# Modulation rows of a two-network kernel: w_mod slabs multiplied on GpSimd ahead of time and kept in a 16-row table

## The chip, the cores and the metric

One NeuronCore of a Trainium2 chip runs the whole program. The metric is the device time of one execution in microseconds (us). The kernel works in fp32; many matmuls take their operands as fp32r, split into a high and a low part.

## What is computed

The reference chains two blocks over x of 256 tokens by 1024. The first block (hgrn/forgetting attention, differential attention, two mixtures of 32 experts) is not touched. The second block has two layers (MLA and GQA attention, then Hyena), each steered by modulation rows, which are what the change is about:

```python
silu_c = jax.nn.silu(c)                                # c: 1024 numbers
for i in range(2):
    m_l = silu_c @ w_mod[i] + b_mod[i]                 # w_mod[i]: 1024 x 6144
    sh1, sc1, g1, sh2, sc2, g2 = split(m_l, 6)         # six rows of 1024
    hl = rmsnorm(x, norm1_g[i]) * (1 + sc1) + sh1
    ol = mixer(hl)                                     # attention (0), Hyena (1)
    x = x + g1 * ol
    x = x + g2 * mlp(rmsnorm(x, norm2_g[i]) * (1 + sc2) + sh2)
x = rmsnorm(x, final_g)
```

w_mod is 24 slabs of 1024 x 512 (2 MB each, 50 MB in all) that serve one matrix-vector product each. In layer 0 the context tokens get a shift and scale of their own too.

## The kernel before

Weights pass through a ring of six SBUF slots (`RING`), a slab of 128 x 4096 fp32 each: `view_k` shows it as 8 tiles of 128 x 512, tile k holding rows 128k to 128k+127 of the weight. SyncE (SP) loads slabs in a written-out order (lines 680 to 786). Slab n goes to slot n mod 6 and its load waits until the last PE unit that reads slab n - 6 has filled its bank (`plan.last_reader`). A unit is one filling of one of the eight PSUM banks; `make_plan` (line 181) hands out banks in turn, and PE waits before each filling (`claim`) until the bank's last filling is drained.

The names: mod0.pre1 are four slabs (shift and scale of layer 0's first norm), mod0.gate1 two (g1), mod0.pre2 four (shift and scale of the second norm), mod0.gate2 two (g2); mod1 likewise. A slab is worked in one of two ways. `c_product` (line 956) lets PE multiply the 8 tiles by a widened c. The other way is `multiply_c` (line 2050) and `sum_up` (line 961): DVE multiplies tile 0 by a column of silu(c) and adds the seven others, multiplied, one after the other (8 instructions of 128 x 512, each waiting for the last) into a buffer `partial`; then one PE matmul with a matrix of ones sums over the 128 partitions and puts the row into all of them:

```python
tell(mm(banks[u.bank][:, :], ones, partial[name][i], start=True, stop=True), u)
```

`add_bias` (line 2035) adds that to the bias row in shift, scale or gate, which GpSimd's queue has loaded before. mod0.pre1 has to serve two different c and is worked both ways. Of mod1.pre1 the first two slabs go by `c_product`, the other two by DVE.

Where this stands in the order: after the attention, DVE's program (from `turn("turn.a_out", xT3)` on) multiplies gate1's two slabs and pre2's first two, adds the gate's bias, multiplies pre2's last two, and goes into `modulated_after` (line 2001): multiply each 128 x 512 result of the projection by gate, add to h, add both biases, then the norm of two tiles. PE meanwhile projects a_out[0], sums gate1, projects a_out[1], sums pre2 (lines 1365 to 1371). Layer 1 does the same round hyena_out. gate2's two slabs are multiplied by DVE inside the MLP, a slab in two halves. mod1.pre1 comes after layer 0's MLP.

The attention stages that the change reaches: PE projects mla_cq, mla_ckv, gqa_q and gqa_kv, waits for DVE's `lora_ready` (lines 1308 and 2555), transposes, projects mla_q and mla_kv, waits for `mla_qk` (lines 1331 and 2593), and goes through 16 steps of MLA and 16 of GQA (`attend`, line 928; `full_attend`, line 2158). Each step has logits, turned probabilities and an output. In Hyena, PE makes filters, six hyena_in projections with transposes, and twice a DFT, a product on DVE and an inverse DFT.

GpSimd issues small loads (bias rows, gains, tables, lines 796 to 860) and computes nothing.

## Time and profile before

| | us |
|---|---|
| median of 3 runs (2672.91 to 2678.48) | 2678.41 |
| the profiled execution, its own time | 2672.54 |
| its span, first to last instruction | 2670.5 |
| PE, DVE, ACT busy in it | 2363.5, 1976.6, 1341.9 |
| mean granted TensorE clock | 0.933 |

Times below are us from the span's start in that execution. A row of the timeline has its start, its duration, the engine, the line of the kernel, the operation, what it writes and reads, and the count of instructions merged in it; in brackets is how long the engine had stood idle before it and what released it. PE is TensorE's matmuls, SPq the queue of SyncE. A fp32 matmul leaves two records.

### The profile page before, as it was taken

The page shows a single profiled execution, that of the slowest core. Times are in us where ns is not written, and L with a number is a line of the kernel's source. Part 1 is how long each engine was busy: PE and PEld are TensorE (multiplying, and loading weights), DVE is VectorE, ACT ScalarE, POOL GpSimd, SP SyncE. Part 2 cuts the span into 40 slices and gives each one's busy share as a digit, 9 for nine tenths or more (in the row PEclk, how much of TensorE's full clock was granted, in tenths as well). Part 3 has the DMA queues.
Part 4 walks back from the last instruction along what each step waited for, and adds up shares of the span by engine and source line. Part 5 has one row for each costly group of instructions (what it writes and reads, how often), then busy time and mean ns, then how long its engine had stood idle before and what let it go on. Part 6 is the DMA issues. An engine that isn't in the chain of part 4 may idle for free.

```text
span 2670.5 us, 29901 instructions
## 1 busy us (share of the span) xinstructions
PE 2363.5 (89%) x10986; PEld 1734.1 (65%) x10986; DVE 1976.6 (74%) x2443; ACT 1341.9 (50%) x1477; POOL 23.9 (1%) x45
## 2 busy tenths in 40 slices
PE   7996999999988869999999987897999568876998
PEld 6556777777764537777777754563887226733887
DVE  3747999999984649999999983458775644369775
ACT  3235888888861427888888831351432011101432
POOL 0000000000000000000000000000000000000000
PEclk9997999999999978999999997899899678988999
DMA  8314998888883217988888882306465501307370
GB/s 321 126 63 163 380 368 360 360 361 361 361 343 104 95 63 279 365 361 360 361 360 361 361 290 93 131 1 227 167 254 196 190 32 63 126 8 262 133 275 16
DMA packets 116505, 607.80 MB, mean 228 GB/s; under 512 B 5300, under 2 KB 8428, under 8 KB 91644
## 3 DMA queue, kind: packets, MB, share of 16 engines
q1 hardware_dynamic: 111536, 588.83, 56.8%
q0 software_dynamic: 4880, 17.76, 1.9%
q8 instruction: 60, 0.98, 0.2%
q14 instruction: 29, 0.24, 0.0%
HBM read 605.51 MB, written 1.05 MB: 227 GB/s over the span
## 4 chain that ended last, share of the span: by engine, by line
PE 54%; DVE 22%; issue 13%; ACT 9%; DVEq 1%; DMA 0%; POOL 0%; SPq 0%; ACTq 0%
PE bank L900 10%; DVE slab_parts L2393 6%; ACT high L1695 5%; PE bank L912 4%; PE bank L1174 4%; PE bank L1126 3%; PE bank L1153 3%; PE bank L999 3%; PE bank L1115 3%; PE bank L1387 2%; PE bank L1389 2%; PE bank L1388 2%; PE bank L1400 2%; PE bank L1402 2%; PE bank L1401 2%
## 5 line engine op out<-in xcount | busy, mean ns | idle before, releaser
L2393 DVE TENSOR_TENSOR slab_parts<-ring,high 128x2048 fp32r<-128x2048 f32 x384 | 862.3, 2288 | 41.8 <-ACT high L1695 37.9
L1695 ACT ACTIVATE high<-ring 128x2048 fp32r<-128x2048 f32 x384 | 727.6, 1914 | 44.6 <-PE bank L1126 35.7
L1126 PE MATMUL bank<-high,xT_parts 128*128 128x512 f32 x1024 | 294.3, 409 | 17.9 <-DVE slab_parts L2393 14.1
L1126 PE MATMUL bank<-slab_parts,xT_parts 128*128 128x512 f32 x1024 | 279.0, 394 | 0.0
L1538 ACT ACTIVATE arena<-bank 128x512 f32<-128x512 f32 (+4 forms) x162 | 89.4, 586 | 357.7 <-PE bank L900 98.8
L900 PE MATMUL bank<-ring,xT 128*128 128x512 f32 (+3 forms) x576 | 237.7, 574 | 11.1 <-DVE xT L2025 7.1
L1126 PEld LDWEIGHTS bank<-high,xT_parts 128*128 128x128 f32 x1024 | 184.7, 190 | 78.7 <-DVE slab_parts L2393 38.5
L1126 PEld LDWEIGHTS bank<-slab_parts,xT_parts 128*128 128x128 f32 x1024 | 193.5, 189 | 45.5
L1701 ACT ACTIVATE arena<-bank 64x512 f32<-64x512 f32 (+2 forms) x352 | 184.7, 534 | 62.8 <-PE bank L1153 52.1
L900 PEld LDWEIGHTS bank<-ring,xT 128*128 128x128 f32 x576 | 111.0, 194 | 134.5 <-issue 122.9
L1558 ACT ACTIVATE high<-ring 128x2048 fp32r<-128x2048 f32 x64 | 121.8, 1912 | 87.7 <-PE bank L1402 82.2
L2612 DVE TENSOR_TENSOR slab_parts<-ring,high 128x2048 fp32r<-128x2048 f32 x64 | 146.1, 2291 | 20.7 <-ACT high L1558 20.3
L1153 PE MATMUL bank<-high,hidden_parts 128*128 128x512 f32 x512 | 151.3, 417 | 7.0 <-DVE hidden_parts L2415 4.7
L1387 PE MATMUL bank<-xT_parts,high 128*128 128x256 f32 x512 | 148.1, 289 | 10.2 <-DVE slab_parts L2612 10.2
L1389 PE MATMUL bank<-xT_parts,slab_parts 128*128 128x256 f32 x512 | 145.7, 285 | 0.0
L1388 PE MATMUL bank<-xT_low,high 128*128 128x256 f32 x512 | 145.5, 284 | 0.0
L1153 PE MATMUL bank<-slab_parts,hidden_parts 128*128 128x512 f32 x512 | 141.5, 398 | 0.0
L1143 PEld LDWEIGHTS bank<-arena 128*128 128x128 f32 x1024 | 121.8, 192 | 5.9 <-ACT arena L1701 3.1
L1143 PE MATMUL bank<-arena 128*128 128x64 f32 x1024 | 123.0, 273 | 2.3 <-ACT arena L1701 2.3
L1701 ACT ACTIVATE xT_parts<-bank 128x512 fp32r<-128x512 f32 x128 | 76.3, 598 | 85.3 <-PE bank L1115 83.8
L1174 PE MATMUL bank<-arena 128*128 128x512 f32 x256 | 115.2, 592 | 2.7 <-DVE arena L2423 2.7
L885 PE MATMUL bank<-resident,arena 128*128 128x128 f32 x208 | 43.3, 384 | 83.6 <-DVE arena L1970 39.2
(361 smaller groups left out, 3679.1 us busy)
## 6 DMA issues: line engine op xcount, KB each, us to landing
ring<-in_moe_w_gate SPq DMA_DIRECT2D x64, 2048.0 KB, 8.5
ring<-in_moe_w_up SPq DMA_DIRECT2D x64, 2048.0 KB, 9.2
ring<-in_moe_w_down SPq DMA_DIRECT2D x64, 2048.0 KB, 8.8
ring<-in_mlp_w SPq DMA_DIRECT2D x32, 2048.0 KB, 13.4
ring<-in_w_mod SPq DMA_DIRECT2D x24, 2048.0 KB, 8.0
ring<-in_even_w_in SPq DMA_DIRECT2D x7, 2048.0 KB, 21.5
ring<-in_odd_w_in SPq DMA_DIRECT2D x6, 2048.0 KB, 10.1
ring<-in_h_w_in SPq DMA_DIRECT2D x6, 2048.0 KB, 7.9
```

The source lines that it names most:

```text
L900: last = mm(banks[u.bank][:, 0:n], lhs(k, tile), w[:, k, c0:c0 + n], start=(k == 0), stop=(k == k_tiles - 1))
L1126: last = mm(dst[:, :], seated2[:, 4 * half + k, e], part_[:, k, :], start=(half == a == k == 0), stop=(half == a == 1 and k == 3))
L1143: last = mm(dst[:, (4 * w + f) * SEATS:(4 * w + f + 1) * SEATS], raw[:, w, f * P:(f + 1) * P], fold, start=True, stop=True)
L1153: last = mm(dst[:, :], hidden2[:, f], part_[:, f, :], start=(a == f == 0), stop=(a == 1 and f == 3))
L1174: ins = mm(banks[bank][:, :], weightedT[:, (j // 2) * P:(j // 2 + 1) * P], pair_y[:, (j % 2) * 512:(j % 2 + 1) * 512], start=first, stop=last)
L1387: mm(dst, w_high[:, k, fs], xT_high[:, k, :], start=(k == 0), stop=False)
L1388: mm(dst, w_high[:, k, fs], xT_low[:, k, :], start=False, stop=False)
L1389: last = mm(dst, w_low[:, k, fs], xT_high[:, k, :], start=False, stop=(k == KD - 1))
L1695: act_fn(hi, weight_half(layer, name, half), ACT.Copy).then_inc(sem(f"high{layer}"), 1)
L1701: act_fn(dst, src(banks[u.bank]), func).then_inc(done or moe_drained[layer][u.bank], 1)
L2393: v.tensor_tensor(low, w, hi.bitcast(F32), ALU.subtract).then_inc(sem(f"low{layer}"), 1)
L2612: v.tensor_tensor(w_low, loaded, w_high.bitcast(F32), ALU.subtract).then_inc(sem("mlp_low"), 1)
```

## The change

Of the 24 slabs the four of mod0.pre1 stay as they are. The other twenty are split in two groups, mods_a (12) and mods_h (8), and are loaded and multiplied long before their rows are used. GpSimd multiplies a slab in the ring, in place: 8 multiplications of 128 x 512 by a column of silu(c), then sums of the first half and the second half of the tiles (4, 2 and 1 tiles wide), every instruction waiting for the one before. DVE does this for mod0.gate1's two slabs by the old chain, its result now in the slab's tile 0. PE then takes two slabs together (`collect`): a matmul with a 16-column one-hot matrix puts each slab's sum into its own row of a 16 x 512 PSUM tile, and DVE adds that tile to the table `mod_rows` (`keep`). Where the row is used, `spread` copies table row n to all partitions with one matmul.

The six collects of mods_a stand: before the wait for lora_ready, before the wait for mla_qk, after MLA steps 7 and 14, after GQA step 9, and before the transposes ahead of layer 0's MLP. The four of mods_h: before hyena_in, after its round 4, and after each DFT. The slabs' slots are freed by their collects, and the load order and GpSimd's program change with it. In `modulated_after` the biases and the scale now come ahead of the projection's results. mod1.pre1's c_products and the widening of c before them are gone.

```diff
+MODS = {"mods_a": tuple((name, i) for name, n in (("mod0.gate1", 2), ("mod0.pre2", 4), ("mod0.gate2", 2), ("mod1.pre1", 4))
+                        for i in range(n)),
+        "mods_h": tuple((name, i) for name, n in (("mod1.gate1", 2), ("mod1.pre2", 4), ("mod1.gate2", 2))
+                        for i in range(n))}
+ON_VECTOR = (("mod0.gate1", 0), ("mod0.gate1", 1))
+HYENA_SLABS = ("hyena_in", "hyena_in", "mod1.gate1", "mod1.gate1", "mod1.pre2", "hyena_in", "hyena_in", "hyena_in",
+               "hyena_in", "mod1.pre2", "mod1.pre2", "mod1.pre2", "mod1.gate2", "mod1.gate2")
+SUMS_AT = {("mla", 7): 2, ("mla", 14): 3, ("gqa", 9): 4}
...
         @block.sync
...
-            for name in ("gqa_q", "gqa_kv", "mla_q", "mla_kv", "mod0.gate1",
-                         "a_out", "mod0.pre2"):
+            for name in ("gqa_q", "gqa_kv", "mla_q", "mla_kv", "mod0.gate1", "mod0.pre2", "mod0.gate2", "mod1.pre1",
+                         "a_out"):
                 stream(name)
...
         @block.gpsimd
...
+                    for k in range(KD):
+                        link(nc.gpsimd.tensor_scalar(w[:, k], w[:, k], silu_c[:, k:k + 1], None, ALU.mult))
+                    for n in (4, 2, 1):
+                        link(nc.gpsimd.tensor_tensor(w[:, 0:n], w[:, 0:n], w[:, n:2 * n], ALU.add))
...
             load("rope2d_loaded", rope2d, A["rope2d"])
+            pool.wait_ge(sem("c_silu"), 1)
+            multiply_c("mods_a")
             pool.wait_ge(sem("gqa_o"), 16)
             load("bias0_gate1", gate, A["b_mod"][0, 2 * D:3 * D].partition_broadcast(P))
...
             gain_row(8)
+            multiply_c("mods_h")
             gain_row(9)
...
         @block.tensor
...
+            def collect(group, g):
+
+                u = U[group][g]
+                claim(u)
+                for a in range(2):
+                    n = 2 * g + a
+                    name, i = MODS[group][n]
+                    if (name, i) in ON_VECTOR:
+                        pe.wait_ge(sem(name + ".partial"), i + 1)
+                    else:
+                        pe.wait_ge(sem("mod_step"), POOL_STEPS * (ON_POOL.index((name, i)) + 1))
+                    last = mm(banks[u.bank][0:16, :], hot[:, 15 - n:31 - n], view_k(slab_ap(K[name][i]), KD, 512)[:, 0],
+                              start=(a == 0), stop=(a == 1))
+                tell(last, u)
+
+            def spread(u, name, i):
+
+                n = MODS[MOD_GROUP[name]].index((name, i))
+                drained(pe, U[MOD_GROUP[name]][4 if name in ("mod0.gate1", "mod0.pre2") else -1])
+                claim(u)
+                tell(mm(banks[u.bank][:, :], ident[0:16, n:n + 1].to_broadcast([16, P]), mod_rows, start=True, stop=True), u)
...
+            pe.wait_ge(sem("hot_ready"), 1)
+            collect("mods_a", 0)
             pe.wait_ge(sem("lora_ready"), 1)
...
+            collect("mods_a", 1)
             pe.wait_ge(sem("mla_qk"), 1)
...
                 if i == 0:
                     for k in range(2):
-                        sum_up(U["mod0.gate1"][k], "mod0.gate1", k)
-            for k in range(4):
-                sum_up(U["mod0.pre2"][k], "mod0.pre2", k)
+                        spread(U["mod0.gate1"][k], "mod0.gate1", k)
+                    for k in range(4):
+                        spread(U["mod0.pre2"][k], "mod0.pre2", k)
...
-            pe.wait_ge(sem("c_wide_ready"), 2)
-            for i in range(2):
-                c_product(U["mod1.pre1"][i], K["mod1.pre1"][i], 0)
-            for i in range(2, 4):
-                sum_up(U["mod1.pre1"][i], "mod1.pre1", i - 2)
+            for i in range(4):
+                spread(U["mod1.pre1"][i], "mod1.pre1", i)
...
         @block.vector
...
             def modulated_after(name, gate, bias):
 
                 g = gain_row()
+                add_bias(bias, [shift, scale], bias.replace("mod", "bias").replace(".", "_"), 2)
+                link(v.scalar_tensor_tensor(scale, scale, 1.0, g, ALU.add, ALU.mult))
...
+            def keep(group, g):
+
+                u = U[group][g]
+                full(dve, u)
+                if g == 0:
+                    drain(v.tensor_copy(mod_rows, banks[u.bank][0:16, :]), u)
+                else:
+                    drain(v.tensor_tensor(mod_rows, mod_rows, banks[u.bank][0:16, :], ALU.add), u)
...
             tell(v.tensor_copy(stat[:, 165:166], z_ckv[:, 0:1]), "lora_ready")
+            for i in range(2):
+                multiply_c("mod0.gate1", i)
+            keep("mods_a", 0)
             dma_done(dve, "rope2d_loaded")
...
             turn("turn.a_out", xT3)
-            for i in range(2):
-                multiply_c("mod0.gate1", i, i)
-            for i in range(2):
-                multiply_c("mod0.pre2", i, i)
             add_bias("mod0.gate1", [gate], "bias0_gate1", 1)
-            for i in range(2, 4):
-                multiply_c("mod0.pre2", i, i)
             modulated_after("a_out", gate, "mod0.pre2")
```

## Rows read from the trace of the kernel before

**Rows 1.** The page, busy time, share of the span and instructions of each engine

```profile
PE 2363.5 (89%) x10986; PEld 1734.1 (65%) x10986; DVE 1976.6 (74%) x2443; ACT 1341.9 (50%) x1477; POOL 23.9 (1%) x45
```

**Rows 2.** Timeline of DVE, layer 0's output projection

```profile
1818.81 0.49 DVE L2058 TENSOR_SCALAR rows<-ring,small 128x512 f32<-128x512 f32 x1
...
1824.84 0.49 DVE L2058 TENSOR_SCALAR rows<-ring,small 128x512 f32<-128x512 f32 x1
...
1842.94 1.41 DVE L2043 TENSOR_TENSOR arena<-arena,bank 128x512 f32<-128x512 f32 x2
...
1857.90 0.69 DVE L2010 TENSOR_TENSOR arena<-bank,arena 128x512 f32<-128x512 f32 x1
...
1862.40 2.86 DVE L2043 TENSOR_TENSOR arena<-arena,bank 128x512 f32<-128x512 f32 x4
1865.29 1.22 DVE L2015 SCALAR_TENSOR_TENSOR arena<-arena,gain 128x1024 f32<-128x1024 f32 x1
...
1869.33 0.16 DVE L1962 RECIPROCAL stat<-stat 128x1 f32<-128x1 f32 x1
...
1872.10 0.15 DVE L1980 COPY stat<-gain 128x1 f32<-128x1 f32 x1
```

**Rows 3.** Timeline of PE, the same stretch

```profile
1819.40 13.97 PE L900 MATMUL bank<-ring,xT 128*128 128x512 f32 x32 [0.99 <-ACT xT L1538]
1833.21 1.88 PE L965 MATMUL bank<-rows,resident 128*128 128x512 f32 x4
...
1857.29 3.75 PE L965 MATMUL bank<-arena,resident 128*128 128x512 f32 x4 [6.75 <-DVE arena L2010]
```

**Rows 4.** Waits in layer 0's MLP, 1876 to 2066: us, times, longest

```profile
PE bank L1387 <- DVE slab_parts L2612: 5.1, 1, 5.1
```

**Rows 5.** Timeline of PE, MLA steps 7 and 8 (outputs)

```profile
1749.38 1.00 PE L952 MATMUL bank<-arena 128*128 128x64 f32 x8
...
1751.58 1.00 PE L952 MATMUL bank<-arena 128*128 128x64 f32 x8
```

**Rows 6.** Groups of DVE instructions, 2100 to 2230: count, busy us, mean ns

```profile
L2700 DVE RECIPROCAL rows<-rows 128x1024 f32<-128x1024 f32 x2 | 13.1, 6552 | 10.8 <-ACT rows L1869 10.8
...
L2696 DVE TENSOR_TENSOR arena<-arena 128x2048 f32<-128x2048 f32 x4 | 9.2, 2293 | 12.4 <-PE bank L1442 12.3
```

**Rows 7.** Line 2060, multiply_c: ns min/median/max, first and last start

```profile
L2060 DVE SCALAR_TENSOR_TENSOR arena<-ring,small,arena x84: 750/752/753, 1575.8 to 2449.8; 128x512 f32<-128x512 f32 x84
```

**Rows 8.** Timeline of PE, the transposes after lora_ready

```profile
1699.45 1.54 PE L1313 MATMUL bank<-resident,arena 128*128 128x128 f32 x6 [9.00 <-DVE stat L2555]
```

**Rows 9.** Stretches, PE's sums of rows 3 after their wait

```profile
core 0: us, PE busy (x) PEld busy (x) DVE busy (x) ACT busy (x) POOL busy (x), PEclk, DMA share, GB/s
...
1857.30:1861.00 3.70, 3.70 (x4) 1.08 (x4) 3.53 (x7) 0.01 (x1) 0.00 (x0) 0.50 1.03 408
```

**Rows 10.** Timeline of SyncE's queue, slab loads

```profile
1713.69 121.80 SPq L689 DMA_DIRECT2D ring<-in_w_mod  x4
```

**Rows 11.** The page, DMA issues: count, size, median us to landing

```profile
ring<-in_w_mod SPq DMA_DIRECT2D x24, 2048.0 KB, 8.0
```

**Rows 12.** Timeline of DVE, mod1.pre1

```profile
2069.80 0.14 DVE L2656 COPY stat<-stat 128x1 f32<-128x1 f32 x1
...
2090.32 1.22 DVE L2668 SCALAR_TENSOR_TENSOR arena<-arena,gain 128x1024 f32<-128x1024 f32 x1
```

**Rows 13.** DMA issues, 2070 to 2072

```profile
arena<-in_b_mod POOLq DMA_DIRECT2D x2, 512.0 KB, 5.1
```

**Rows 14.** Timeline of PE, hyena_in and the first inverse DFT

```profile
2230.86 27.79 PE L912 MATMUL bank<-xT,ring 128*128 128x256 f32 x128
...
2351.11 3.78 PE L1487 MATMUL bank<-arena 128*128 128x512 f32 x4 [7.26 <-DVE xT L2746]
```

**Rows 15.** Groups of instructions, DVE, 2325 to 2412

```profile
L2743 DVE TENSOR_TENSOR arena<-rows 128x512 f32<-128x512 f32 x8 | 5.5, 692 | 0.3
```

More of the change, by code:

```diff
@@ L169, in mlp @@
             if j in GATE_SUMS:
-                self.sum_up(gate, GATE_SUMS.index(j), (0,))
+                self.take(gate, 1, (0,))
             if j < MLP_STEPS:
@@ L228, in make_plan @@
     p.stream("mla_kv", 1, 8)
+    for name, _ in MODS["mods_a"]:
+        p.vector_slabs(name, 1)
+    p.take("mods_a")
     p.take("mla_qT", 4)
@@ L239, in make_plan @@
         if i == 0:
-            for k in range(2):
-                p.sum_up("mod0.gate1", k)
-    p.vector_slabs("mod0.pre2", 4)
-    for k in range(4):
-        p.sum_up("mod0.pre2", k)
+            p.take("mod0.gate1", 2)
+            p.take("mod0.pre2", 4)
+    p.take("mods_a")
     p.take("turn.n2_0", 4)
     p.mlp("mlp0", "mod0.gate2")
-    p.stream("mod1.pre1", 2, 1)
-    p.vector_slabs("mod1.pre1", 2)
-    for k in range(2, 4):
-        p.sum_up("mod1.pre1", k)
+    p.take("mod1.pre1", 4)
     p.take("turn.n1_1", 4)
+    p.slab("filter_w4", None)
+    for name in HYENA_SLABS:
+        p.slab(name, None)
     p.take("filter_mlp", 3)
@@ L271, in make_plan @@
         if i == 0:
-            for k in range(2):
-                p.sum_up("mod1.gate1", k)
-    p.vector_slabs("mod1.pre2", 4)
-    for k in range(4):
-        p.sum_up("mod1.pre2", k)
+            p.take("mod1.gate1", 2)
+            p.take("mod1.pre2", 4)
     p.take("turn.n2_1", 4)
     p.mlp("mlp1", "mod1.gate2")
+    p.read_by_sums()
     return p
@@ L602, in build @@
         gate = at(14336, 1024)
-        two, four = [rows[:, 512 * i:512 * (i + 1)] for i in range(2)], [at(16384 + 512 * i, 512) for i in range(4)]
-        partial = {"mod0.pre1": four, "mod0.gate1": two, "mod0.pre2": four, "mod0.gate2": two, "mod1.pre1": four,
-                   "mod1.gate1": two, "mod1.pre2": four, "mod1.gate2": two}
+        four = [at(16384 + 512 * i, 512) for i in range(4)]
+        partial = {"mod0.pre1": four}
+        mod_rows = routers[0:16, 0:512]
+        hot = w_fox_f[:, 0:31]
         silu_c = small[:, 464:472]
```

107 lines of the change are left out of this document (61 added, 46 removed).

## Prediction

> **What bounds the kernel now.** I read the page first: TensorE (PE) is busy for 89% of the span and VectorE (DVE) for 74%, GpSimd (POOL) for 1% [rows 1]. An average says little here, so I then read the timelines of the stages that the change touches. In layer 0's output projection DVE starts the first w_mod slab at 1818.81 and the second at 1824.84: 6.03 us a slab, six slabs, 36.2 us, and the normalised tiles are ready at 1872.10 [rows 2]. PE projects a_out within the same time, then stands 6.75 us for DVE [rows 3]. So DVE sets the end there, and layer 1 repeats the pattern. In the two MLPs it is otherwise: PE waits once, 5.1 us at the start, and never again in 190 us [rows 4], so the two slabs that DVE multiplies inside each MLP cost nothing now and their removal gives nothing. In the attention steps PE has no gap: step after step begins 2.20 us apart [rows 5]. Whatever is put on PE there costs its full time.
>
> **Step 1, price of a slab on GpSimd.** Eight multiplications of 128x512 and sums of 128x2048, 128x1024 and 128x512, each waiting for the one before. The trace has no such work on POOL. Lower bound: DVE's price for the shapes, 8 x 0.49 + 2.29 + 1.22 + 0.69 = 8.1 us, 8.6 with gaps of 0.04. Upper bound: every element at the dearest DVE rate, the reciprocal's 6552 ns for 1024, or 6.4 ns; 7680 elements make 49 us [rows 2, 6]. The true value I expect near the lower end, since these are ordinary additions: I take 0.75 us, DVE's row for 512 elements of two operands [rows 7], for each multiplication, and twice DVE's time for each sum, 6.0 + 8.4 = 14.4, rounded to T = 14.
>
> The Trainium skill's page "GPSIMD Engine Reference" (section 3.1, Elementwise) gives 4497 ns for GpSimd's 128x2048 sum and 769 ns for a 512-element loop; by it a slab would be about 14.2 us, an estimate, and no run here shows it.
>
> **Step 2, the two DVE slabs before the attention.** DVE now tells lora_ready and PE, after 9.00 us of waiting, transposes at 1699.45 [rows 8]. The changed PE first needs table sum 0, whose two slabs DVE multiplies after lora_ready: 12.1 us. The two one-hot matmuls are like two ones-matmuls, 1.88 us for four records at full clock (2.4 GHz) and 3.75 us at granted clock 0.50 (the 1.2 GHz level), after a 6.75 us wait [rows 3, 9]. Behind a 21 us wait they should be slow: 3.75. Together +15.9. The DVE work up to mla_qk follows the same delay (its 0.7 us copy of the sum into the table included), and table sum 1 ends as that is ready. So the attention begins 16 us late.
>
> **Step 3, table sums inside the attention, and the wait for GpSimd.** The third and fourth pre2 slabs go into slots freed by mla_q and mla_kv. The first is issued at 1713.69 now [rows 10], after the change at 1729.6, and lands 8.0 us later [rows 11], 1737.6. GpSimd had been idle, so from there it works slab after slab: slab k is done at 1737.6 + kT. Table sum 2 (after MLA step 7, 1750.4 + 16 = 1766.4) needs two: 1765.6, just in time; it ends at 1768.3. Table sum 3 (after step 14) is reached seven steps on, 1768.3 + 15.4 = 1783.7, and needs four: 1793.6. PE waits 10 us; the sum ends at 1795.5. From the end of step 14 now (1765.8) to the start of the a_out projection at 1819.40 are 53.6 us [rows 3, 5]; with 1.9 for table sum 4 (slab 6 is done at 1821.6, PE comes at 1827) the projection starts at 1851.0: **+31.6**. In general this is 4T - 24.4, but not under 21.6 (T up to 11.5). GpSimd's queue also carries the loads of gate, shift and scale, now behind slab 8: 1849.6, landed by 1857, before they are needed at 1867. A return to full clock after the 10 us wait: +2.
>
> **Step 4, layer 0's output projection.** The chain of six slabs goes. PE: a_out's first half 14.0, six spreads at 0.86 = 5.2. Its second half would follow, but it reuses banks that DVE drains only after the gate and both modulation adds (1.4 + 2.9) and scale's 1.22: it starts about 22 us after the first instead of 15.5, and takes 13.9. Then two adds (1.4), two tiles of normalising at 2.78 [rows 2]: 1819.4 + 21.9 + 13.9 + 1.6 + 5.6 = 1862.4 against 1872.10, **-9.7**. Table sum 5 stands in PE's wait before the transposes: 0, and 1.9 if that wait were gone.
>
> **Step 5, mod1.pre1.** Now DVE has the MLP's result at 2069.80, and reaches the scale at 2090.32 [rows 12], after widening c, two slabs and the c_products. After: the same 2069.80, then the bias loads, which GpSimd issues at that point and which land 5.1 us after the issue [rows 13]; with two issues of about 1 us behind one another I take 2076.5. Four adds (2.9): scale at 2079.4. **-10.9**.
>
> **Step 6, layer 1.** Table sums 0 and 1 of mods_h stand in a gapless run of PE (27.8 us and more): +3.8. Sums 2 and 3 stand before the inverse DFTs, where PE waits 7.26 us for DVE [rows 14]: 0, given GpSimd is done, for which it has about 35 us for the first two slabs, from the landing of their loads on, and 74 for four; cover gone, 1.9 each. DVE's four table adds fall in its waits but the last: 0.2. The output projection as in step 4: **-9.7**. Loads: the slabs come in an order that leaves each hyena_in slab at least 15 us ahead of its use: 0; if one came late, its 8 us landing would show.
>
> **Step 7, both engines at the SBUF.** No row has GpSimd and DVE computing together. Lower bound 0: DVE's steps beside DMA traffic into the ring hold 750 to 753 ns [rows 7]. Upper bound: every two-input DVE instruction beside GpSimd doubles, some 20 us before the attention (1691 to 1711) and in the Hyena stage 11 us (products of two SBUF tiles as in line 2743, four groups of eight, half of them beside GpSimd) and 6 us of the convolution: 37 [rows 15]. I take 7, near the undisturbed rows.
>
> **Sum** for the profiled execution: 31.6 + 2 - 9.7 - 10.9 + 4.0 - 9.7 + 7 = +14.3, say **+14**. Its own time of 2672.5 becomes 2686.5. The median of the runs shown is 5.9 above that execution, so the forecast for the median is 2678.4 + 14 = **2692**. About 0.2% (5.4 us) is what a measurement can tell from no change.
>
> **Rivals.** *A, GpSimd is quick enough.* If a slab takes under 11.5 us, no table sum is waited for (21.6 instead of 31.6, and no clock loss), the engines don't disturb each other, and the sums inside the attention fit beside the exps rather than adding 5.6. Then 21.6 - 5.6 - 9.7 - 10.9 + 4 - 9.7 = -10: 2668. For it: DVE does the shapes in 8.6. Against: PE's steps show no gap. With the attention's sums exposed it ends at -4.7, 2674, no change. Chance 0.30 for both, 0.14 for the faster one. *B, the memory is contended.* All 37 us are lost: +44, 2722. Chance 0.17. *C, GpSimd is slower.* T = 18: step 3 gives 47.6, the biases land 7 us late for the gate: +37, 2715. Chance 0.13. The forecast's own case, T from 12 to 16: 0.40, and 2680 to 2705.
>
> The Trainium skill's page "SBUF — State Buffer" (section Who interferes with whom) speaks against the change: GpSimd shares a port pair with DVE, a DVE copy or tensor_scalar in a two-port mode and a GpSimd instruction exclude each other for a whole instruction, and a two-input DVE instruction contends with GpSimd's reads. By that rule B or worse would come; no row here has the two together.
>
> **How the numbers follow.** The range runs from A's unchanged end, 2671, to B's, 2725, and leaves out the faster half of A and T above 19. Faster by over 0.2%: A's faster half, 0.14. Within 0.2%: the rest of A and the low edge of the forecast's case, 0.20. Slower: 0.66.
>
> **What would show it.** POOL rows of 128x512 near 0.75 us and 128x2048 near 4.6; PE waiting about 21 us before the transposes of cq, and about 10 us for POOL at the fourth table sum; the a_out stage near 43 us in place of 53; PE's spreads at 0.86; DVE's 0.69 and 0.75 us rows unstretched outside POOL's time. Wrong would be: POOL slabs under 11 or over 17 us, DVE rows beside POOL at 1 us and more, or a table sum waited for in the Hyena stage.

## Result, and the profile after

| us | before | after |
|---|---|---|
| median, runs taken side by side (4 each) | 2676.17 | 2785.39 (2778.70 to 2787.11) |
| ratio, 95% interval | | 1.0404 [1.0382, 1.0427] |
| span of the profiled execution | 2670.5 | 2785.2 |
| mean granted TensorE clock | 0.933 | 0.908 |

Slower by 4%, where +14 us had been forecast. "Before" and "after" are the two kernels from here on. The page of the kernel after, the line that answers to [rows 1]:

```profile
PE 2409.4 (87%) x10998; PEld 1755.5 (63%) x10998; DVE 1955.5 (70%) x2326; ACT 1342.4 (48%) x1477; POOL 411.2 (15%) x243
```

VectorE (DVE) lost 117 instructions but only 21 us of busy time. The difference between the spans, laid out by stage, with the issues of the bias loads in GpSimd's (POOL's) queue as marks (an issue waits for the end of a stage); the forecasts are those of the prediction's steps 2 to 6, whose last 7 us (step 7, GpSimd beside DVE) it gave to no stage; the last column is the kernel with GpSimd's arithmetic left out, e1 below:

| stage | before | after | change | forecast | e1 |
|---|---|---|---|---|---|
| up to the end of the second mixture of experts | 1573.65 | 1581.28 | +7.6 | 0 | 1573.68 |
| to the end of the attention | 243.03 | 343.93 | +100.9 | +33.6 | 262.19 |
| layer 0's output projection | 55.99 | 45.42 | -10.6 | -9.7 | 51.61 |
| MLP 0 | 197.57 | 197.68 | +0.1 | 0 | 197.90 |
| mod1.pre1 | 27.40 | 15.91 | -11.5 | -10.9 | 15.91 |
| Hyena | 314.62 | 348.20 | +33.6 | +4 | 314.58 |
| hyena_out | 55.28 | 49.47 | -5.8 | -9.7 | 49.47 |
| the rest | 202.96 | 203.31 | +0.4 | 0 | 203.26 |

The 7.6 us of the first line lie in untouched code and vary from run to run (1573 to 1580 in the kernels below). In after the attention's end is marked late: the issue stands behind GpSimd's last slab. By TensorE's (PE's) own rows the a_out projection starts 95.7 us late (1922.70 against 1819.40, less 7.6), and from there to the MLP's first matmul it is 5.3 us shorter.

**GpSimd's prices.** Groups of POOL instructions in after: count, busy us, mean ns, idle before:

```profile
L836 POOL TENSOR_SCALAR ring<-ring,small 128x512 f32<-128x512 f32 x144 | 235.4, 1635 | 214.7 <-DMA ring<-in_w_mod 201.6
L838 POOL TENSOR_TENSOR ring<-ring 128x2048 f32<-128x2048 f32 x18 | 82.0, 4555 | 1.5
L838 POOL TENSOR_TENSOR ring<-ring 128x1024 f32<-128x1024 f32 x18 | 43.3, 2403 | 1.4
L838 POOL TENSOR_TENSOR ring<-ring 128x512 f32<-128x512 f32 x18 | 26.9, 1494 | 1.4
```

The sums cost twice DVE's time, as taken. The multiplication, of one tile by a column, cost 1635 ns and not 750. A slab that met no disturbance took 13.15 + 8.25 us and the gaps, 21.6 from its start to that of the next. Timeline of POOL in after, one such slab and the starts of three sums further up:

```profile
1707.75 8.64 POOL L838 TENSOR_TENSOR ring<-ring 128x2048 f32<-128x2048 f32 x3
...
1731.22 9.14 POOL L838 TENSOR_TENSOR ring<-ring 128x2048 f32<-128x2048 f32 x3
...
1764.34 8.24 POOL L838 TENSOR_TENSOR ring<-ring 128x2048 f32<-128x2048 f32 x3
...
1816.98 13.15 POOL L836 TENSOR_SCALAR ring<-ring,small 128x512 f32<-128x512 f32 x8
1830.22 8.25 POOL L838 TENSOR_TENSOR ring<-ring 128x2048 f32<-128x2048 f32 x3
```

**DVE beside it.** Timeline of DVE in after: four instructions that began within 0.7 us behind the start of a sum (the first three sums above, and one in Hyena that began at 2454.53), and between them a row of six beside GpSimd's multiplications (1722.45):

```profile
1708.09 4.44 DVE L2123 TENSOR_SCALAR ring<-ring,small 128x512 f32<-128x512 f32 x1
...
1722.45 5.61 DVE L2125 SCALAR_TENSOR_TENSOR ring<-ring,small 128x512 f32<-128x512 f32 x6
...
1731.91 3.87 DVE L2646 TENSOR_SCALAR rows<-rows 128x64 f32<-128x64 f32 x1
...
1764.44 4.54 DVE L2667 COPY arena<-arena 128x256 f32<-128x256 f32 x1
...
2454.58 4.99 DVE L2817 TENSOR_TENSOR xT<-rows 128x512 f32<-128x512 f32 x1
```

The durations of the four are 0.49, 0.20, 0.29 and 0.69 us where nothing disturbs them. Each ends about when the first of the three sums (4555 ns in the mean) is over. Beside GpSimd's multiplications, which read one tile, DVE is touched far less: the six of 1722.45 take 5.61 us, 4.69 undisturbed, a fifth more.

**PE waits.** Timeline of PE in after, up to the output projection:

```profile
1721.94 1.86 PE L1015 MATMUL bank<-ring,w_fox_f 128*16 128x512 f32 x2 [23.70 <-DVE ring L2127]
1729.20 1.89 PE L1015 MATMUL bank<-ring,w_fox_f 128*16 128x512 f32 x2 [5.39 <-DVE ring L2127]
...
1777.24 6.89 PE L960 MATMUL bank<-resident,arena 128*96 128x128 f32 x48 [19.21 <-DVE arena L2673]
...
1838.52 1.89 PE L1015 MATMUL bank<-ring,w_fox_f 128*16 128x512 f32 x2 [20.43 <-POOL ring L838]
...
1881.74 1.03 PE L1015 MATMUL bank<-ring,w_fox_f 128*16 128x512 f32 x2 [2.40 <-POOL ring L838]
...
1922.70 16.12 PE L935 MATMUL bank<-ring,xT 128*128 128x512 f32 x32 [0.99 <-ACT xT L1602]
1938.75 5.41 PE L1024 MATMUL bank<-routers,resident 16*128 16x512 f32 x12
1947.08 15.87 PE L935 MATMUL bank<-ring,xT 128*128 128x512 f32 x32 [2.92 <-DVE arena L2076]
```

The first two stand in the place of the 9.00 us of [rows 8]; the third, at the heads' transposes, was 1.72. Some of the waits go with a low clock as well. Stretches of after, busy us of each engine, granted clock, DMA share, GB/s:

```profile
1700.00:1730.00 30.00, 2.66 (x3) 0.27 (x4) 27.97 (x25) 0.30 (x1) 28.63 (x16) 0.53 0.18 68
1760.00:1780.00 20.00, 2.76 (x13) 2.63 (x14) 17.12 (x23) 1.19 (x2) 19.19 (x10) 0.58 1.05 390
1820.00:1850.00 30.00, 11.48 (x43) 8.66 (x43) 2.74 (x9) 2.46 (x5) 28.54 (x17) 0.52 0.29 100
1880.00:1920.00 40.00, 37.49 (x127) 26.84 (x128) 10.93 (x35) 8.79 (x20) 38.09 (x22) 0.53 0.29 106
```

In the first three PE hardly works. In the last it works almost without a gap, but at the lower of its two clock levels, behind a wait of 2.40 us; in the kernel before, the same steps ran at the higher one. From the heads' transposes to the first matmul of the a_out projection are 90.3 us before, 96.0 in e1 and 145.5 after.

### The profile page after: what moved, and what is told of

Same layout as the page of the kernel before. It is cut to its first block and busy times, and to the rows that moved or that the text cites. A ratio compares the mean times of both kernels' runs of the same rounds, so it can differ in the third digit from the quotient of the medians.

```text
span 2785.2 us, 30024 instructions
## 1 busy us (share of the span) xinstructions
PE 2409.4 (87%) x10998; PEld 1755.5 (63%) x10998; DVE 1955.5 (70%) x2326; ACT 1342.4 (48%) x1477; POOL 411.2 (15%) x243
## 5 line engine op out<-in xcount | busy, mean ns | idle before, releaser
L836 POOL TENSOR_SCALAR ring<-ring,small 128x512 f32<-128x512 f32 x144 | 235.4, 1635 | 214.7 <-DMA ring<-in_w_mod 201.6
L935 PE MATMUL bank<-ring,xT 128*128 128x512 f32 (+3 forms) x576 | 244.2, 586 | 16.9 <-DVE xT L2089 7.1
L810 POOL DMA_DIRECT2D arena<-in_b_mod x14 | 8.1, 580 | 1060.1 <-DVE stat L2441 772.0
L838 POOL TENSOR_TENSOR ring<-ring 128x2048 f32<-128x2048 f32 (+2 forms) x54 | 152.2, 2818 | 4.3
```

Of the source, the lines that this page charges most:

```text
L836: link(nc.gpsimd.tensor_scalar(w[:, k], w[:, k], silu_c[:, k:k + 1], None, ALU.mult))
L838: link(nc.gpsimd.tensor_tensor(w[:, 0:n], w[:, 0:n], w[:, n:2 * n], ALU.add))
L935: last = mm(banks[u.bank][:, 0:n], lhs(k, tile), w[:, k, c0:c0 + n], start=(k == 0), stop=(k == k_tiles - 1))
```

## Experiments

Twelve kernels. Those named e change the kernel after to find the cause, those named b look for a version that beats both. The ratios are against runs of the kernel before taken beside them, whose medians were 2674.29 (e1 to e4), 2673.61 (e5, e6, b1), 2674.32 (b2, b3), 2673.54 (b4, b5) and 2673.47 (e7). Each diff of an e is against the kernel after; b1's is against the kernel before, those of b2 to b5 are against the b that the text names, and they show the main lines.

**e1: GpSimd's arithmetic left out** (its 18 slabs enter the table unmultiplied).

```diff
             pool.wait_ge(sem("c_silu"), 1)
-            multiply_c("mods_a")
...
-                        pe.wait_ge(sem("mod_step"), POOL_STEPS * (ON_POOL.index((name, i)) + 1))
+                        slab_in(K[name][i])
```

> The changed kernel with GpSimd's multiplications left out: the table sums take tile 0 of the 18 slabs as it was loaded, PE waits for the landing alone (so those rows of the output's modulation are not computed). Theory G (all of the loss is GpSimd's slab time and its disturbance of DVE): the step sum without GpSimd is +21.6 before the a_out projection, -11.5 in mod1.pre1, about -5.5 in each output projection as measured after, +4 in Hyena, so near the kernel before: 2670 to 2690. Theory L (the order of the loads, the slots held longer, the table sums and the spreads themselves cost the time): it stays above 2720.

Measured: 2672.25, ratio 0.9991 [0.9980, 1.0001]. Timeline of PE in e1:

```profile
1705.84 1.86 PE L1013 MATMUL bank<-ring,w_fox_f 128*16 128x512 f32 x2 [15.11 <-DVE ring L2125]
1711.78 1.89 PE L1013 MATMUL bank<-ring,w_fox_f 128*16 128x512 f32 x2 [4.08 <-DVE ring L2125]
...
1742.30 5.45 PE L958 MATMUL bank<-resident,arena 128*96 128x128 f32 x48 [1.85 <-DVE arena L2671]
```

All that the change does beside GpSimd's arithmetic comes to nothing: 19 us lost before and in the attention, given back in the two projections and mod1.pre1. The 113 us between e1 and the kernel after come with GpSimd's arithmetic.

**e2: four of eight products** (the others left out).

```diff
-                    for k in range(KD):
+                    for k in range(KD // 2):
```

> The changed kernel with only four of eight multiplications in each GpSimd slab; the sums stay (half of each slab's products are left out). A slab falls from 21.6 to about 15.0 us, with the long 128x2048 sum still there. Theory W (the attention's loss is waiting, 4 slabs by 6.6): -26 in the attention, about -20 in Hyena where two waits vanish, a few less in DVE's stretched chain: 2730 to 2745. Theory C (what costs is that the sums hold DVE up, not the slab's length): at most -15, so above 2765.

Measured: 2731.98, ratio 1.0216 [1.0199, 1.0233]. A slab is 6.5 us shorter, 118 us over the 18, and 53 us came back. Of these 47 lie between the heads' transposes and the a_out projection (98.2 us against 145.5): PE's waits for POOL there fall from 22.8 us to 0.5, and the granted clock stays at 1.00. So far this fits "PE waits until GpSimd is done". But e2 is still 60 us above e1 although hardly a wait is left for POOL. In the attention PE's long waits are for DVE:

```profile
PE bank L1015 <- DVE ring L2127: 32.5, 2, 21.4
PE bank L960 <- DVE arena L2673: 12.1, 1, 12.1
```

**e3: pre2's first two slabs left out on GpSimd**, so that nothing disturbs DVE before the attention.

```diff
+LEFT_OUT = (("mod0.pre2", 0), ("mod0.pre2", 1))
...
-                    if (name, i) in ON_VECTOR:
+                    if (name, i) in ON_VECTOR + LEFT_OUT:
                         continue
```

> The changed kernel, but GpSimd leaves the first two pre2 slabs unmultiplied, so it computes nothing while DVE normalises and turns before the attention; all later slabs as in the changed kernel. Theory C (GpSimd's instructions hold DVE's up): DVE's chain there, about 22 us longer than its own durations, returns to them, the attention and with it the loads for the later slabs start that much sooner: 2785 minus 18 to 25, 2760 to 2767. Theory W (only the length of GpSimd's slabs matters, and these two were never waited for): no change, 2780 to 2787.

Measured: 2778.29, ratio 1.0389 [1.0372, 1.0406]. Waits of PE in the attention stages:

```profile
PE bank L1018 <- POOL ring L839: 36.6, 4, 20.5
PE bank L1018 <- DVE ring L2130: 19.2, 2, 15.1
PE bank L961 <- DVE arena L2676: 5.1, 1, 5.1
```

Between the two forecasts; the 7 us below the kernel after are hardly clear of its own spread (2778.70 to 2787.11), so the stages have to say what happened. Before the attention PE's waits for DVE are back to e1's 15.1 + 4.1, with 5.1 at the heads where e1 has 1.9, and the attention begins 24 us sooner. PE then waits for GpSimd, 36.6 us in place of 22.8, and the a_out projection starts 10 us sooner. Before the attention the hold on DVE decides, inside it GpSimd's pace; a gain at the one is mostly lost at the other.

**e4: gate1's two slabs multiplied before the norm of cq**, in the 41 us in which DVE is idle. Nothing left out.

```diff
+            for i in range(2):
+                multiply_c("mod0.gate1", i)
             for u in U["mla_cq"]:
                 drained(dve, u)
...
-            for i in range(2):
-                multiply_c("mod0.gate1", i)
             keep("mods_a", 0)
```

> The changed kernel with DVE multiplying gate1's two slabs before the norm of cq, in the 41 us in which DVE waits for ACT, instead of after lora_ready. Same work, same results. Theory P (the place of these two slabs costs 12 us plus what GpSimd stretches them by): PE's waits of 23.7 and 5.4 us before table sum 0 go, but GpSimd's second slab (done at 1740.5) is then waited for by table sum 1 and limits it: 14 to 24 us less, 2761 to 2771. Rival (the wait only moves, since GpSimd sets the pace of the attention anyway): less than 5 us.

Measured: 2766.58, ratio 1.0339 [1.0321, 1.0356]: 19 us back, inside the forecast. The attention begins 16 us sooner and the a_out projection 14 (the stretches ahead of it taken off). The long waits that stay are for GpSimd, and at the heads for the DVE that it disturbs:

```profile
PE bank L1015 <- POOL ring L838: 35.1, 4, 19.6
PE bank L960 <- DVE arena L2673: 19.9, 1, 19.9
```

Two theories were left, pace (how long GpSimd has a slab) and lock (its two-input sums hold DVE). Three kernels were made to tell them apart.

**e5: products only**, the three sums left out.

```diff
-                    for n in (4, 2, 1):
-                        link(nc.gpsimd.tensor_tensor(w[:, 0:n], w[:, 0:n], w[:, n:2 * n], ALU.add))
```

> Left out: GpSimd's three sums per slab (so the rows made from its slabs hold only the first of eight products). GpSimd's time per slab falls from 21.6 to 13.3 us, 150 us less over 18 slabs, and nothing is left on GpSimd that has two inputs. Theory pace (only GpSimd's time per slab counts; halving the products took 118 us from GpSimd and 53 from the span, 0.45 of it): 2785 - 0.45 x 150 = 2718, range 2708 to 2730. Theory lock (the sums cost more than their length, because a VectorE instruction that meets one is held until it ends): VectorE's chain before the attention and in Hyena returns to its own durations (0.49, 0.29, 0.69 us rows where 4.4 to 5.0 stand now), and the span falls below 2705, down to 2680.

Measured: 2701.00, ratio 1.0102 [1.0087, 1.0118]. Below what pace gives, and where lock puts it. Timeline of DVE in e5, beside GpSimd's products (1.23, 4.69, 0.23 and 0.17 us undisturbed):

```profile
1700.33 1.62 DVE L2000 TENSOR_TENSOR arena<-arena,rows 128x1024 f32<-128x1024 f32 x1
...
1710.15 5.65 DVE L2123 SCALAR_TENSOR_TENSOR ring<-ring,small 128x512 f32<-128x512 f32 x6
...
1738.20 0.51 DVE L2153 TENSOR_TENSOR arena<-arena 128x64 f32<-128x64 f32 x1
...
1739.68 0.63 DVE L2152 TENSOR_TENSOR arena<-arena 128x16 f32<-128x16 f32 x1
```

So the products hold DVE too, but by less than half a us at a time and not for their 1.64 us.

But 19 of e5's 29 us above e1 are neither pace nor lock. From the heads' transposes to the a_out projection e5 takes 115.3 us, e1 96.0, and within that stretch PE waits for the same things and as long in both. What differs is the clock. Ten us of the second attention in e5 (busy us of PE, PEld, DVE, ACT and POOL, granted clock, DMA share, GB/s):

```profile
1820.00:1830.00 10.00, 10.00 (x34) 6.76 (x32) 2.82 (x9) 2.59 (x7) 9.44 (x7) 0.50 0.01 2
```

and ten us of it in e1:

```profile
1800.00:1810.00 10.00, 10.00 (x58) 6.62 (x56) 5.25 (x17) 5.06 (x12) 0.00 (x0) 1.00 0.01 2
```

It was 0.50 for some 37 us, with PE busy throughout. e6 and e7 have the same (115.2 and 114.9 us). GpSimd at work is neither enough for it, since e2 keeps its clock there, nor needed, since b1 below loses it with GpSimd idle.

**e6: the eight products as one two-input instruction**; same result.

```diff
-                    for k in range(KD):
-                        link(nc.gpsimd.tensor_scalar(w[:, k], w[:, k], silu_c[:, k:k + 1], None, ALU.mult))
+                    link(nc.gpsimd.tensor_tensor(w, w, over(silu_c, [P, KD, 512], 2), ALU.mult))
```

> The eight products of a slab (8 x 1.635 us) become one tensor_tensor of 128x4096 with the eight scalars read 512 times each; the sums stay, the result is the same. By the sum of 128x2048 in 4.555 us the product should take 9.1 us, so a slab 17.4 us instead of 21.6. Theory pace: 18 x 4.2 us x 0.45 = 34 us less than 2785, so 2751, range 2740 to 2765. Theory lock: every GpSimd instruction now has two inputs, and the product holds a VectorE instruction up to 9 us; the span is then no shorter than 2775, up to 2830, with single VectorE rows of 6 to 9 us beside the product.

Measured: 2883.78, ratio 1.0788 [1.0771, 1.0804], 98 us above the kernel after, although a slab takes 15.4 us of GpSimd and not 21.6. In e6, the product among the groups of POOL:

```profile
L835 POOL TENSOR_TENSOR ring<-ring,small 128x4096 f32<-128x4096 f32 x18 | 126.6, 7036 | 320.3 <-DMA ring<-in_w_mod 319.4
```

The timeline of POOL:

```profile
1767.93 7.02 POOL L835 TENSOR_TENSOR ring<-ring,small 128x4096 f32<-128x4096 f32 x1
```

The timeline of DVE:

```profile
1767.96 7.01 DVE L2151 TENSOR_TENSOR arena<-arena 128x16 f32<-128x16 f32 x1
...
1775.22 4.36 DVE L2153 TENSOR_TENSOR arena<-arena 128x16 f32<-128x16 f32 x1
```

The longest wait of PE:

```profile
PE bank L959 <- DVE arena L2672: 86.6, 1, 86.6
```

A DVE instruction of 128x16, 0.17 us by itself, takes 7.01. DVE's rotations, some 50 small instructions, are let through a few between two GpSimd instructions, and PE waits 86.6 us for their end. Nowhere in e6 does PE wait for POOL. Pace alone can't explain this kernel; the hold on DVE can. (Pace still counts where PE does wait for POOL, as in the attention of the kernel after and of e3.)

**e7: sums only**, the products left out.

```diff
-                    for k in range(KD):
-                        link(nc.gpsimd.tensor_scalar(w[:, k], w[:, k], silu_c[:, k:k + 1], None, ALU.mult))
```

> Left out: GpSimd's eight products per slab (its slabs are summed unmultiplied). The counterpart of the kernel with the products alone: there a slab held GpSimd for 13.3 us and the span was 2701; here it holds it for 8.4 us, all of it in instructions with two inputs. Theory pace (what counts is how long GpSimd has a slab): shorter than with the products alone, 2672 to 2701. Theory lock (what counts is that a two-input instruction of GpSimd holds up VectorE): longer than with the products alone though the slabs are ready sooner; the three sums stand against every VectorE chain they meet, 2672 + (2785 - 2701) = 2756 if nothing overlaps, range 2715 to 2760, with VectorE rows of 4 to 5 us where 0.2 to 0.7 is their own.

Measured: 2752.94, ratio 1.0288 [1.0270, 1.0305]. The slabs are ready 5 us sooner than e5's and the kernel is 52 us slower, 3 below lock's sum of 2756. In Hyena GpSimd now begins while DVE brings the filter's angles into range; its timeline there:

```profile
2147.69 25.06 POOL L836 TENSOR_TENSOR ring<-ring 128x2048 f32<-128x2048 f32 x9
```

DVE's, where 0.28 and 0.42 us are their undisturbed durations:

```profile
2152.42 2.37 DVE L2160 TENSOR_SCALAR arena<-arena 64x256 f32<-64x256 f32 x1
...
2156.16 4.67 DVE L2162 SCALAR_TENSOR_TENSOR arena<-arena 64x256 f32<-64x256 f32 x1
```

And PE's waits for the convolution and for the filter's steps, 6.3 and 4.0 us at most in the kernel before:

```profile
PE bank L1524 <- DVE stat L2793: 28.1, 1, 28.1
PE bank L1482 <- ACT small L1925: 26.1, 2, 21.3
```

The totals add up: 2672.3 (neither), + 28.8 (products), + 80.7 (sums) = 2781.8, against 2785.4. By stage they don't, so the agreement is luck. Above e1, without the stretch ahead of the change:

| us above e1 | e5, products | e7, sums | both added | after |
|---|---|---|---|---|
| to the heads' transposes | 6.4 | 23.8 | 30.2 | 27.3 |
| from there to the a_out projection | 19.3 | 18.9 | 38.2 | 49.4 |
| Hyena | 3.2 | 40.3 | 43.5 | 33.6 |

The middle row is the fallen clock in e5 and e7, and in the kernel after the waits for POOL (22.8) with the low clock behind them. The first and last rows are the hold on DVE: about 10 us for the products, 64 for the sums.

**b1: everything on DVE, where it was idle.** The table stays, GpSimd computes nothing, and the rows are spread before a_out's first projection.

```diff
                         tell(v.tensor_reduce(neg_max[:, s % 2, 0, 0:1], banks[u.bank][:, :], AX_X, ALU.max,
                                              negate=True), name + "_max")
+                        multiply_c("mod0.pre2", s // 8 + (2 if name == "gqa" else 0), None, (s % 8, s % 8 + 1))
...
+                    if w == 0 and half == 1:
+                        for q in range(7 * j, 7 * j + 7):
+                            m, k = divmod(q, KD)
+                            if m < len(mods) and mods[m]:
+                                mod, i = mods[m]
+                                multiply_c(mod, i, gate_partial[i] if "gate2" in mod else None, (k, k + 1))
...
+            for k in range(2):
+                spread(U["mod0.gate1"][k], "mod0.gate1", k)
+            for k in range(4):
+                spread(U["mod0.pre2"][k], "mod0.pre2", k)
             for i, idx in enumerate(K["a_out"]):
```

> A version meant to beat both. Nothing on GpSimd. VectorE multiplies all slabs, in place, where its row showed it idle: layer 0's gate1 in the 41 us before the norm of cq, pre2's 32 instructions one per step of the two attentions, gate2 and mod1.pre1 seven instructions per MLP step, Hyena's gate1 and pre2 after the sums of the two filters and after the fourth and fifth convolution; the 16-row table stays, and the rows are spread before the first output projection instead of after it. Against before: output projection 4 to 8 us shorter (after had 5.3, and the 2.9 us wait for a bank goes), mod1.pre1 11.5 shorter, hyena_out 6 to 9 shorter; more: two collects of 1.9 us in layer 0's attention, two in Hyena, four of 0.95 in the MLP, 11 in all. Sum 2674 - 13 = 2661, range 2652 to 2675. Rival: VectorE's added instructions delay the steps of the attention or the MLP (48 instructions in the MLP leave 28 us of 190 idle): then 2675 to 2700, and PE waits for VectorE appear in the MLP or in the attention.

Measured: 2735.38, ratio 1.0229 [1.0215, 1.0243], above its forecast and its rival's. The projections, mod1.pre1 and Hyena came out as expected (48.97, 15.88, 312.40, 49.41). Three stages did not: the attention 276.07 (+33), MLP 0 239.32 (+42) and the rest 214.8 (+12), which holds layer 1's MLP. In MLP 0 PE waits 31 us for DVE, and ScalarE (ACT) 17.7 us for weights, 2.8 before. The attention is the clock, all but the 4 us of its collects. The same stretch in b1:

```profile
1785.00:1845.00 60.00, 60.00 (x191) 40.54 (x189) 26.10 (x65) 17.05 (x40) 0.00 (x0) 0.50 0.03 12
```

and in b2, below:

```profile
1785.00:1845.00 60.00, 58.19 (x259) 33.42 (x259) 35.59 (x83) 17.70 (x40) 2.10 (x4) 0.94 0.48 176
```

PE is busy throughout in both, and goes through 191 records at the lower level, 259 at the higher. In b1 it fell at 1780, after the collect between the two attentions, the heads' transposes and a wait of 1.11 us, and it stayed there till the stage ended. The kernel before has the same wait and keeps its clock.

**b2: b1 with both collects inside the second attention** (after its steps 4 and 17), and a slab of the MLP multiplied and collected within one step.

```diff
+SUMS_AT = {("gqa", 4): 1, ("gqa", 17): 2}
...
+                    m = j - 1 if w == 0 else j
+                    if half == 1 and 0 <= m < len(mods) and mods[m]:
+                        mod, i = mods[m]
+                        multiply_c(mod, i, gate_partial[i] if "gate2" in mod else None, (4 * w, 4 * w + 4))
```

> The version on VectorE alone again, with the two places mended at which it lost: in the grouped-query attention TensorE ran at a granted clock of 0.50 for 70 us after the first collect had been put between the two attentions, so both collects go inside that attention (its steps 4 and 17); and a w_mod slab held its place in the ring for two MLP steps, which kept the weights behind it back, so a slab is multiplied and collected within one step. If both readings hold: the attention costs 4 us more than before (two collects), output projection 7 less, MLP plus the four collects 4 more, mod1.pre1 11.5 less, Hyena 2 less, hyena_out 6 less (the last three as the last version had them): 2674 - 19 = 2655, range 2648 to 2662. If three slabs per MLP step are too much for the loads whatever the hold, the MLP of layer 0 stays 10 to 40 us longer: 2665 to 2700.

**b3: b2, but mod1.pre1 as in the kernel before**, so that the MLP has the two gate slabs alone.

```diff
-    p.take("mod1.pre1", 4)
+    p.stream("mod1.pre1", 2, 1)
+    p.vector_slabs("mod1.pre1", 2)
```

> As the other kernel of this call, but mod1.pre1 is made as in the kernel before (two slabs by TensorE, two by VectorE, after the MLP), and the MLP carries the two gate slabs alone. What is left of the change is the table for gate1 and pre2 of both layers, multiplied by VectorE where it was idle. Attention 4 more, output projection 7 less, Hyena 2 less, hyena_out 6 less: 2674 - 11 = 2663, range 2657 to 2670. If the granted clock falls in the attention again: 2695 to 2705.

Measured: b2 2736.08, ratio 1.0237 [1.0223, 1.0250]; b3 2700.13, 1.0086 [1.0072, 1.0100]. In both the attention is mended (246.74 and 246.81, +3.8 as computed) and layer 0's projection is 46.79, 9.2 shorter. The MLPs are not: b2 265.76 and 24.7 more in the rest, and b3, with only the gates in them, still 215.41 and 18.3 more in the rest. That b1's slabs kept the weights back was read rightly (ACT's wait for weights is gone in b2), and yet MLP 0 is 26 us longer than in b1, and the kernel lies above both ranges given for it. b3 lies in the range given for a fallen clock, but by luck, since its clock didn't fall. The waits of PE in b2's MLP 0:

```profile
PE bank L998 <- DVE ring L2112: 30.0, 4, 7.5
PE bank L988 <- DVE rows L2112: 14.8, 2, 7.4
```

DVE's last four products stand behind its other work of the step, and PE comes to each sum 7.4 us before they are done. The kernel before ends them a step earlier. In the attention b2 moved the collects and with them the slab loads that wait for them, so which of the two gave the clock back isn't shown.

**b4: b3 with gate2's products where the kernel before has them** (their slabs are also loaded a step earlier).

```diff
-                    m = j - 1 if w == 0 else j
-                    if half == 1 and 0 <= m < len(mods) and mods[m]:
-                        mod, i = mods[m]
-                        multiply_c(mod, i, gate_partial[i] if "gate2" in mod else None, (4 * w, 4 * w + 4))
+                    for m in (j, j - 1):
+                        if w == 0 and half == 1 and 0 <= m < len(mods) and mods[m]:
+                            mod, i = mods[m]
+                            multiply_c(mod, i, gate_partial[i], (4 * (j - m), 4 * (j - m) + 4))
```

> The version with the table for gate1 and pre2 alone, now with gate2's multiplications where the kernel before has them (four instructions in each of two MLP steps, ended a step ahead of the sum). In the last version TensorE waited 7.4 us at each of the sums and the two MLPs were 18 us longer each. By its stages with the MLPs as before: attention +3.8, output projection -9.2, mod1.pre1 -1.0, Hyena -1.6, hyena_out -5.9: 2674 - 14 = 2660, range 2655 to 2666. If the MLPs lose for another reason (slabs of pre2 that lie differently in the ring): 2675 to 2697.

**b5: b2 with the eight products in a row**, ended half a step before the sum.

```diff
-                    m = j - 1 if w == 0 else j
-                    if half == 1 and 0 <= m < len(mods) and mods[m]:
+                    m = j - 1
+                    if w == 0 and half == 1 and 0 <= m < len(mods) and mods[m]:
                         mod, i = mods[m]
-                        multiply_c(mod, i, gate_partial[i] if "gate2" in mod else None, (4 * w, 4 * w + 4))
+                        multiply_c(mod, i, gate_partial[i] if "gate2" in mod else None)
```

> As the other one, and mod1.pre1 by table too; each of the six slabs in the MLP is multiplied by eight VectorE instructions in a row after the step's first two parts and summed at the start of the next step, half a step later. mod1.pre1 10.5 us less than by the two c_products, four collects 3.8 more: 2653, range 2648 to 2662, if VectorE's 6.2 us in a row are covered by the four parts that it is ahead. If three slabs per step overload the loads or VectorE: PE waits in the MLP of 2 to 8 us per step, 2665 to 2700.

Measured: **b4 2659.42 (2655.60 to 2661.63), ratio 0.9943 [0.9929, 0.9957]**, faster than both kernels (than the kernel before by 0.6%, little but clear of the noise) and on the forecast of 2660; b5 2694.72, ratio 1.0079 [1.0065, 1.0093]. Timeline of PE in b4's output projection, against [rows 3]:

```profile
1829.36 6.54 PE L1007 MATMUL bank<-routers,resident 16*128 16x512 f32 x12 [0.99 <-ACT xT L1592]
1835.83 29.93 PE L921 MATMUL bank<-ring,xT 128*128 128x512 f32 x64
```

The spreads come first, and both halves of the projection run without a gap: the 2.92 us wait for a bank, which the order of the kernel after brought, is gone. b4's stages, in the order of the table above from the attention on: 246.88, 46.79, 196.97, 27.05, 310.24, 49.40, 202.71. b5's MLP 0 is 228.95, with waits of PE for DVE of 20 us and a mean clock of 0.92 where the kernel before has 0.96. Its rest is 18.4 longer than before, with layer 1's two gate slabs alone, and with 13.6 us of PE waits for DVE there: so its order of products and loads costs also where only two slabs are in it. Six slabs in MLP 0 didn't pay in any of the three orders tried (b1, b2, b5); none of them was tried with b4's order of the gates, so whether another would pay is open.

## Why the prediction was wrong

Its sign was right, its size was not: 2692 in a range to 2725, against 2785. Two steps failed, the price of the two engines side by side (step 7) and the price of a slab (step 1). All three signs that the prediction had named for being wrong came: slabs over 17 us, DVE rows beside POOL over 1 us, a table sum waited for in Hyena.

- **Step 7 failed: "Both engines at the SBUF ... I take 7, near the undisturbed rows", upper bound 37.** The bound supposed that a two-input DVE instruction beside GpSimd doubles. It is held for as long as GpSimd's two-input instruction lasts, so a 0.17 us instruction grew to 7.01 (e6), a 0.42 one to 4.67 (e7), and one-input instructions are held too (0.20 to 3.87, 0.29 to 4.54). A factor on DVE's time can't bound that; a bound by GpSimd's own two-input time would have been 18 x 8.4 = 151 us, an estimate. In place of 7, the hold cost about 74 us by e5 and e7 (sums 64, products 10). e2 shows the step failing by itself: its slab takes 15.0 us, near the forecast's 14, PE hardly waits for POOL, and it measures 2731.98. The page "SBUF — State Buffer" of the Trainium skill (section Who interferes with whom) says of a DVE instruction in a two-port mode that the engine that comes second "fully blocks", and of a two-input one that it contends with GpSimd's reads; by that the prediction wrote "B or worse", and priced B at a doubling. Beside GpSimd's two-input instructions these runs go as far as the page's stronger word for both kinds (4.54 us for 0.29, 7.01 for 0.17); beside its one-input products they don't: a copy of 0.29 us took at most 0.74 there in e5, next to products of 1.64. Which mode DVE ran in no row shows.
- **Step 1 failed by half:** T = 21.6 us for 14; the range had left out T above 19. The sums were right (8.3 for 8.4), the product was 1635 ns for 750. The Trainium skill's "GPSIMD Engine Reference" (section 3.1, Elementwise) led to the same 14.2. Its 769 ns were not what this form took, 1635. By step 3's own formula, 4T - 24.4, T = 21.6 gives +62 for +31.6. But the formula holds only while the fourth slab sets the wait. By the same working slab 6 is then done at 1867.2 and PE comes for it at 1857.4, which makes it +72 and the whole 2732, an estimate outside the range too. No run has this price without the hold on DVE.
- **Step 2:** forecast 16 us to the attention's start. By PE's rows at the heads' transposes e1 has 13.2 (1742.30 against 1729.11), after 40.5. The mechanism was right, a little cheaper than forecast; the other 27 us are step 7 again.
- **Step 3:** forecast +31.6 at the a_out projection, measured +95.7. Of it e1 shows 19. The wait at table sum 3 was forecast at 10 and was 20.43; the wait for slab 6 at table sum 4, forecast as 0, was 2.40, and PE's clock then stood at 0.53 for 40 us. The forecast had given the clock 2 us. From the heads to the a_out projection the kernel after is 49.4 us above e1; 22.8 are the waits for POOL, and the other 26.6 are time in which PE mostly worked at the low clock.
- **Step 4 and its copy in step 6:** -9.7 each. Measured -5.3 by PE's rows in layer 0, -5.8 in hyena_out (within 0.2 the same in all e kernels). The mechanism, the wait for a bank with it, was right; two terms were too small. In hyena_out of after the second half starts 24.2 us behind the first, not 21.9 (the six spreads took 7.35 us, not 5.2), and after that wait of 2.93 us it takes 15.60, not 13.9: 4.0 in all. In layer 0 the first half took 16.12 as well.
- **Step 5:** -10.9, measured -11.5.
- **Step 6, the Hyena stage:** +4 for collects. In e1 the two in PE's gapless run cost 1.9 us each and the two before the inverse DFTs lie in waits, as forecast. That e1's stage is no longer than before has another reason: the filter's small weights landed 1.9 us after their issue and not 4.9, and PE's wait for them fell from 5.4 us to 2.2. The +33.6 are GpSimd's: PE waits 20.6 us for POOL at table sums, 14.2 at the longest, and the filters' steps on DVE are held (PE's waits for ACT behind them are 22.2 us, 11.8 before).
- **MLP:** 0, measured +0.1.

Of the rivals, B (contention, 2722) and C (T = 18, 2715) named the two mechanisms but took one at a time, each too small. Both held, and they hit different places, as e3 shows. None had a fall of the clock in the attention, which is 19 us in e5, e6 and e7. The sign came right for the prediction's own reason: waits for GpSimd and the disturbance of DVE outweigh what the projections give back, and e1, without them, is at no change.

## What to carry to other kernels

Before giving work to GpSimd, count its two-input instructions and look at what DVE does in the same stretch: a chain of many small DVE instructions on the critical path is the worst neighbour, since each can be held for one whole GpSimd instruction. If the work has to be there, one-input forms are cheaper for the others even where they are slower for GpSimd (the kernel after against e6), and an idle stretch of DVE itself is cheaper still (e4, b4). And when work is moved ahead, the place where its result is collected is as much a part of the cost as the work: a sum a step too early gave 7.4 us of waiting each time (b3 against b4). Last, when parts are measured by leaving out, compare stage by stage and look at the clock: the totals of e5 and e7 added up, and each held 19 us of a low clock that e1 doesn't have, counted twice in the sum.

## Unexpected in the hardware

- The hold is by instruction: in e6, from 1752 to 1841, two DVE instructions stood beside each slab's GpSimd work for 7.0 to 7.1 and 4.4 to 4.5 us, with the size of the GpSimd instruction (7.02, 4.6) and not of their own, and one or more got through between.
- Beside a one-input product of GpSimd (1.64 us) a DVE instruction is held by less than half a us, with one input or two: 0.28 to 0.73, 0.17 to 0.63 (e5).
- On GpSimd a two-input product whose second input is one number read 512 times took 7036 ns for 128x4096, 1.72 ns for each of the 4096; the one-input product by a column took 3.19 (1635 ns for 512), a sum of two tiles 2.22 (4555 ns for 2048).
- PE's clock can stay low while it is busy: 0.50 over the 60 us from 1785 in b1, with PE busy for all of them. In b1, e5, e6 and e7 it fell about 2 us after the first logits of the second attention, and came back while PE ran a collect. What made it fall there wasn't settled. In all four, slab loads ran at 344 to 407 GB/s just then, where the kernel before loads nothing; but e1 and e2 load at 381 to 407 GB/s at the same place and keep 1.00.
